# Six places for raw weights in place of eight, five for pages of keys in place of four, nine for pages of values in place of eight

## What is computed

```python
aq, ak, av, az, mq, mk, mv, mo, mz, ga, gm, mi, mf = jnp.split(xn @ w_in, points, axis=-1)
```

```python
num = w_inter[..., None] * jnp.einsum('bhtd,bhde->bhte', q, c_prev) + jnp.einsum('bhts,bhse->bhte', s, v)
c_new = a_prev[..., None, None] * c_prev + jnp.einsum('bhs,bhsd,bhse->bhde', a_s, k, v)
```

## Time and profile before

| | us |
|---|---|
| median of three runs | 471.71 |
| the profiled execution, its own time | 471.25 |
| its span, first to last instruction | 469.0 |
| PE busy | 457.2 |
| PE weight load busy | 414.5 |
| VectorE busy | 399.5 |
| ScalarE busy | 289.5 |
| GpSimd busy | 101.1 |

### The profile page before, as it was taken

The page is one execution under the profiler, slowest core; times in us unless marked ns, Lnnn a source line. Parts: engine busy times, 40 slices in busy tenths (PEclk is TensorE's granted clock), DMA queues, the critical chain, the costliest instruction groups (busy, mean ns, idle before and its releaser), DMA issues.

```text
span 469.0 us, 11349 instructions
## 1 busy us (share of the span) xinstructions
PE 457.2 (97%) x3855; PEld 414.5 (88%) x3855; DVE 399.5 (85%) x1618; ACT 289.5 (62%) x486; POOL 101.1 (22%) x181
## 2 busy tenths in 40 slices
PE   7999999999989999999999999999999999999997
PEld 4899899898779898888899888899898898899997
DVE  4898899599999997999899999889999964668861
ACT  4866545676973684995485694666948367324430
POOL 2040421013323313322321242322223110000000
PEclk9999999999999999999999999999999999999999
DMA  8899599759999999999999999999999995457511
GB/s 308 316 362 406 180 358 334 236 152 359 305 412 408 408 363 350 387 404 408 410 368 317 408 414 409 410 369 279 398 413 410 409 361 174 142 173 272 178 52 48
DMA packets 44858, 150.91 MB, mean 322 GB/s; under 512 B 6192, under 2 KB 7796, under 8 KB 44672
## 3 DMA queue, kind: packets, MB, share of 16 engines
q1 hardware_dynamic: 20368, 70.77, 41.2%
q0 software_dynamic: 19008, 67.20, 37.6%
q10 hardware_dynamic: 5424, 12.21, 6.7%
HBM read 137.37 MB, written 12.76 MB: 320 GB/s over the span
## 4 chain that ended last, share of the span: by engine, by line
PE 72%; DVE 15%; ACT 7%; issue 2%; DMA 2%; ACTq 0%; POOL 0%; DVEq 0%; POOLq 0%
PE pj L534 26%; PE pj L537 14%; PE wk L534 8%; PE pa L717 5%; DVE wlo L1071 4%; DVE kpages L1170 4%; PE wk L537 4%; DVE cslot L1254 2%; DMA out_C_s<-cslot 2%; PE wk L487 2%; PE wk L639 2%; ACT whi L818 2%; ACT L838 1%; PE wk L673 1%; PE wk L492 1%
## 5 line engine op out<-in xcount | busy, mean ns | idle before, releaser
L534 PE MATMUL pj<-xn,whi 128*128 128x264 f32 x1328 | 180.8, 289 | 0.8 <-ACT mqT L976 0.7
L534 PEld LDWEIGHTS pj<-xn,whi 128*128 128x128 f32 x1328 | 168.5, 189 | 9.1 <-issue 6.2
L1071 DVE TENSOR_TENSOR wlo<-wraw,whi 128x1024 fp32r<-128x1024 f32 x112 | 137.0, 1227 | 9.6 <-ACT whi L818 9.1
L818 ACT ACTIVATE whi<-wraw 128x1024 fp32r<-128x1024 f32 x112 | 117.8, 1053 | 23.1 <-PE wk L537 12.9
L1170 DVE CUSTOM_DVE_ANT_0 kpages<-kpages,qbc 128x128 f32<-128x128 f32 x512 | 115.4, 291 | 1.2 <-DMA kpages<-in_cache_k 1.1
L537 PE MATMUL pj<-xn,wlo 128*128 128x264 f32 x664 | 94.3, 285 | 3.2 <-DVE wlo L1071 3.2
L537 PEld LDWEIGHTS pj<-xn,wlo 128*128 128x128 f32 x664 | 85.6, 188 | 4.3 <-DVE wlo L1071 4.3
L404 POOL DMA_DIRECT2D kpages<-in_cache_k x64 | 34.3, 535 | 170.2 <-DVE sco L1170 146.2
L404 POOL DMA_DIRECT2D vpages<-in_cache_v x64 | 33.9, 530 | 59.3 <-issue 39.2
L1170 DVE DVE_READ_ACCUMULATOR2_ANT sco<- 128x1 f32 x512 | 42.4, 83 | 0.0
L717 PE MATMUL pa<-vpages,prob 128*32 128x256 f32 x512 | 34.2, 385 | 1.4 <-ACT prob L876 1.4
(11 more groups left out here) (272 smaller groups left out, 620.6 us busy)
## 6 DMA issues: line engine op xcount, KB each, us to landing
wraw<-in_weights SPq DMA_DIRECT2D x112, 512.0 KB, 6.7
kpages<-in_cache_k POOLq DMA_DIRECT2D x64, 512.0 KB, 8.2
vpages<-in_cache_v POOLq DMA_DIRECT2D x64, 512.0 KB, 10.6
cslot<-in_states SPq DMA_DIRECT2D x16, 512.0 KB, 9.4
out_C_s<-cslot ACTq DMA_DIRECT2D x16, 512.0 KB, 8.3
xres<-in_tokens SPq DMA_DIRECT2D x1, 1056.0 KB, 5.7
out_k_p<-kT ACTq DMA_DIRECT2D x4, 256.0 KB, 9.6
out_v_p<-v_nat ACTq DMA_DIRECT2D x4, 256.0 KB, 4.8
```

The source lines that it names most:

```text
L534: mm(bank[:, 0:T], whi[:, q, k, :], src[:, g, k, :], start=(k == 0 and g == 0), stop=False)
L818: A(whi[:, n % WSPLIT], wraw[:, n % WRAW], ACT.Copy).then_inc(whi_ready, 1)
L1071: V.tensor_tensor(wlo[:, n % WRAW], wraw[:, n % WRAW], whi[:, n % WSPLIT], ALU.subtract).then_inc(wlo_ready, 1)
```

## The change

Three constants change. Places and semaphores are made from them, and so are the waits of `load_w`, `keys` and `values`, the number of pages that are issued at the start, and the address of the last value slot. The memory used is the same: two places of 4 KB a partition are taken from the weights, one is given to the keys and one to the values.

```diff
-WRAW = 8
+WRAW = 6
 WSPLIT = 4
 AHEAD = 3
 LOW = AHEAD - 1
 
-KSLOTS = 4
-VSLOTS = 8
+KSLOTS = 5
+VSLOTS = 9
 CSLOTS = NB
```

## The result

The changed kernel takes 474.02 us, median of 13 runs (472.56 to 475.99), and the kernel before 471.67 us (13 runs, 471.17 to 472.20). The ratio is 1.0051, 95% interval 1.0040 to 1.0062: slower by 2.35 us, half a per cent. The profiled execution has a span of 471.9 us, 2.9 us more than that of before, and took 474.02 us.

A forecast was written before the change was run, and what follows sets the result against it. TensorE (PE), busy 97% of the span, was taken as the bound, with the DMA engines as second limit. Terms 1.3 + 0 + 0 + 0 gave +1.3 us: 473.0 us for the median, range 470.9 to 475.1.

The forecast's parts named there:

- Part 1: At L639, pair 3 of states leaves two projections later; PE waits 0.9, 0.4 and 0 us in rounds 1-3, 1.3 us together.
- I cost that round at nothing: Round 0 at L639: DMA engines not full, states' loads land in 6.0 to 6.4 us, so no cost.
- Part 2: At ScalarE's copy L818, weights' lead shrinks from five projections to three; cost nothing, bounds 0 and 1.8 us.
- Part 3: At the start, the put of decay rows queues behind two more pages, 3.0 us later; cost 0, bounds 0 and 2.1 us.
- Who waits for it first?: At the start, PE's transposes of probabilities were to meet VectorE's delay first, with 3.1 us of cover.
- Part 4: VectorE's 1.1 us of waits for keys go, but do not reach the end; gain 0, bounds -1.1 and 0 us.
- The third (start or tail): Rival: rows' put 5.2 us late, PE waits 2.1 us, or a late weight copy costs 1.8 us; 475.1 us, chance 0.09.
- the first: The forecast with its upper bound: PE waits at L639 for states' loads, +1.3 us; chance 0.42.
- Hidden: Rival: all four reads at L639 find pair 3 there; 471.7 us, up to 472.6; chance 0.37 together with inert.
- faster: Rival: fifth key place removes VectorE's 1.1 us of waits at L1170, shortening PE's wlo waits; 470.6 us, chance 0.12.

The follow-up runs named there:

- put ahead: Changed kernel with the fifth key page and eighth value page issued behind the queries' loads, after the put of rows: 474.09 us, ratio 1.0050.
- both edits: Changed kernel with the put of rows behind four key and seven value pages, and states' pairs one group earlier: 471.33 us, ratio 0.9995.

## Why the prediction was right, and where it was not

- **The sum.** Forecast +1.3 us, 473.0 us; measured +2.35 us, 474.02 us, within the range 470.9 to 475.1 and slower as forecast. The sum was 1.05 us short, and it is in part luck that it was not shorter: the states' term was 0.5 us too large by the trace, the start's 1.1 us too small, and a term of 0.4 us in round 1 was not in it at all.
- **Part 1, the states' loads.** Right in mechanism and place: the named instruction waited, in one of the two named rounds. Its size was 1.3 us (0.9, 0.4, 0) and it was 0.8 us (0.8, 0, 0) in the profile. The need was taken 0.1 us too early: the first twenty instructions take 1.1 us, not 1.0. The landing was forecast 10.4 us after the issue of round 1 and came after 10.2; in rounds 2 and 3 11.4 and 10.7 were forecast and 10.8 and 9.9 came. Alone (six places only, or states later only) it measures 0.9 and 1.2 us. "I cost that round at nothing" held for round 0 in the changed kernel; it stopped holding as soon as other pages were moved there (put ahead, 1.1 us).
- **Part 2, the weights.** Right: 0.6 us of ScalarE's waits in all, none of it seen by PE, and the undone pair of costs leaves nothing over. It holds for six places; with five the late copies do reach PE.
- **Part 3, the start.** This is the step that was mis-sized: "I take 3.0 us, near the low end ... Cost 0". The put came back 3.9 us later, and VectorE went on 4.6 us later, since the reading back took longer too, a second transfer in the same queue that the term left out. Less the 0.3 us of the first loads, and against a cover of 3.1 us, that makes 1.2 us by the prediction's own arithmetic and 1.1 us measured. The bounds, 2.6 to 5.2 us of delay and 0 to 2.1 us of cost, held; the value within them was chosen too low. The answer to "Who waits for it first?" was wrong as well: not the transposes but VectorE's own low parts, which took 0.8 of the 1.1 us. The total still comes out of the cover of the transposes, since all these waits have the same lateness of VectorE as their cause and the transposes' cover is the smallest (in the kernel before the three low parts are ready 4.2, 3.9 and 3.5 us before PE takes them). Nor is the delay used up at 84.86 us, where VectorE had only 2.12 us of waiting to give: in the changed kernel its own extra lateness is gone at 94.82 us, at no cost to PE. With the put on another queue all of it goes in the trace (by time 1.6 us less, with the same loads of states).
- **Part 4, what it gives.** Right: VectorE's 1.1 us of waits for keys are gone from the trace and PE's waits for low parts did not shrink (3.7 us after 3.2). The fifth place has a use that I had not seen: in the two kernels with late states and four places for keys VectorE waited 2.0 and 2.2 us for pages.
- **The 2.9 us of the profile** by places: 0.3 us before the first projection, 1.1 us at the start, 0.4 us at low parts in round 1 (below), 0.8 us at L639, and 0.3 us at low parts in rounds 2 and 3 less 0.1 us at the last values. Why those of rounds 2 and 3 came later is open.
- **The rivals.** The third (start or tail) was true beside the first, not in its place; I had given it 0.09 as if it excluded the forecast's small numbers. Its sign, a wait of PE near 82 us for the probabilities, came with 0.3 us; the larger part showed at low parts, where I had looked for no sign. Hidden and faster are both out by the interval.

## What to carry to other kernels

Count buffers as moments of issue: a ring that is one place shorter moves not only its own loads but everything that stands behind them in the same queue, and the load to look at is the one whose reader has no slack. A deeper ring at the start is not free either, if a small transfer that somebody waits for is queued behind its first fill; issue that one first or on another queue. Two such costs can trade places, as they did here, so undo them one at a time and together before calling one of them harmless.

## What was not expected

**VectorE's products are slowed when GpSimd broadcasts beside them.** In round 1 PE lost 0.4 us at low parts in the eight kernels where the broadcasts of the rows (L433, L434) fell on VectorE's scoring of a page. In the kernel before and in that with both edits they fell on the making of a low part, which kept its 1.22 us. The changed kernel, VectorE and GpSimd:

```profile
120.62 0.49 DVE L1170 CUSTOM_DVE_ANT_0 kpages<-kpages,qbc 128x128 f32<-128x128 f32 x1
121.04 0.49 DVE L1170 CUSTOM_DVE_ANT_0 kpages<-kpages,qbc 128x128 f32<-128x128 f32 x1
...
120.33 0.78 POOL L433 PARTITION_BROADCAST decay<-decay  x1 [1.09 <-DMA floor<-rows_dram]
```

Two products take 0.49 us each where 0.29 is the mean of all of this line on the page (0.29 in the kernel before too). In the whole trace of the changed kernel the 506 products beside which no broadcast ran took 0.31 us at most; of the six beside a broadcast three took longer, 0.49, 0.49 and 0.88 us. This is read from traces alone; no kernel moved the broadcast by itself, and GpSimd's spans are rough.

**A short stop costs its own length, a long one more.** The late pair cost PE 0.8 us in the changed kernel, where its weight load waited 0.7 us, and the granted clock stayed full. In the kernel with five places the stops of 4.0 to 5.7 us at L639 cost their own length and 1.7 to 2.8 us more in the matmuls behind them, where the granted clock was 0.50 to 0.69.
